# Where the squares of a projection's tiles are added up: matmul engine or pool engine

## The chip, the cores and the metric

The kernel runs on one core of one Trainium2 chip. The metric is the device time of one execution, in microseconds (us). The kernel before takes 815.71 us, the median of 3 runs (815.12 to 815.75).

## The reference, cut to what matters

A sequence of 256 tokens with 16 extra tokens in front of it, 1024 channels wide, in float32, passes through two blocks. The first block is a feed-forward network, an mLSTM mixer and a second feed-forward network; the second block is two layers of dilated attention beside a gated convolution. Every part ends in the same way: an output projection, an RMS norm of its result with a gain per channel, and an addition to the stream h.

```python
h = h + 0.5 * rmsnorm(swiglu(rmsnorm(h, gn[0]), ffn_w_in[i, 0], ffn_w_out[i, 0]), gn[1])
u = rmsnorm(h, gn[2])
y = mlstm_mixer(u, ...)                    # ends in: y @ w_out
h = h + rmsnorm(y, gn[3])                  # the first output projection of the change
h = h + 0.5 * rmsnorm(swiglu(rmsnorm(h, gn[4]), ffn_w_in[i, 1], ffn_w_out[i, 1]), gn[5])
# then, for l in 0, 1
mix = jnp.concatenate([att, cnv], axis=-1) @ w_out[l]
x = x + gate[:, None, :] * rms_norm(mix, post_norm_g[l])   # l = 0: the second one of the change
```

`rmsnorm(y, g)` needs, for each token, the sum over the 1024 channels of y². The kernel also wants the norm of the *next* part without waiting for the new h: the mean of (h + r·g·y)² is the mean of h² + 2r·mean(h·g·y) + r²·mean(g²·y²), where r is the first norm's factor. So at each boundary three sums per token are formed: of y², of (g·y)² and of h·g·y.

## The kernel before, in words

Channels lie on the 128 partitions and tokens on the free axis: h is `hT`, 8 tiles of 128 channels by 272 tokens. A weight chunk is 128 x 1024 floats. It arrives by DMA in `raw` (5 slots), and `advance` (L189) splits it into a high part `w1`, copied by ScalarE (ACT), and a low part `w2`, which VectorE (DVE) gets by a subtraction of two SBUF operands (`w<-raw,w`). Each product takes three matmuls, w1·x1, w1·x2 and w2·x1. A block of 128 output channels over 8 input tiles is thus 24 matmuls of 256 tokens. `advance` is called ahead of use: when block j is issued, the split of the chunk four further on goes into the queues of ACT and DVE.

The kernel's order is written out by hand. Each engine has one list (`Eng`, whose `replay` is the line L110 or L112 of nearly every instruction in the profile), is served in that order, and waits for semaphores of the others. TensorE (PE) runs the matmuls, GpSimd is called POOL here, and SyncE (SP) issues the DMAs.

An output projection is `row_of_tiles` (L279). For the feed-forward networks it has 22 input tiles for each of 8 output tiles; for the mixers it has 8. In the mixers' case `head` (L233) does the first three output tiles together, ending one right after the other, and `block` (L264) does one at a time after that. A block can call a function in its middle, `mid`, before its seventh input tile (after 18 of its 24 matmuls).

After each output tile k, `evac_tile` (L399) reads it from PSUM `ps`. In all cases ACT writes g·y into `yg`, and DVE multiplies it by h (`hyg`) and adds that to the running `sqa[2]`. For the squares there are two ways.

- *Row sums on PE* (not `pooled`: both mixers' projections). ACT writes y² into `sq`. `column_sums` (L384) then makes `sq` the stationary operand of a small matmul per 128 tokens, against two columns of `wts`: 1/D and g²/D. So one square serves both sums. A float32 matmul is two PE instructions, so that a tile's row sums are four. They wait in the list `late` and are issued in the middle of the next block; those of the last tile follow its square.
- *Gathered on POOL* (`pooled`: both feed-forward networks). ACT writes two squares, of y into `sq` and of g·y into `sqg`. POOL adds each into a running sum, `sqa[0]` and `sqa[1]`. `early_sums` (L459) sums both over the partitions, in eight small PE instructions, in the middle of the last tile. There PE waits for POOL's additions of the seventh tile. For the last tile only y² is formed and summed with both weights.

After the last tile, `rms_first` (L485) reads the sums, POOL takes the power -1/2, and PE spreads the factor over the partitions (`spread`, L478). Then `add_and_weigh` (L608, after the mixer) or `add_and_normalise` (L579, layer 0) updates h and makes the operands of the next `head`. `dense` issues filler matmuls for waits of PE.

The queues of DVE and ACT in a mixer's projection, from tile 3 on, are: for each block the split of a chunk, then the evacuation of that block's tile. The split that is queued with block 7 stands in front of the evacuation of tile 7. Ahead of tile 3's evacuation stand the splits of three chunks (numbered 5, 6, 7, counting the projection's own from 0), the first of which block 5 needs. The chunks up to 11 are split by the end of the projection.

Of the kernel before, what the change touches and what calls it, by code (L numbers as in the profile page):

```python
# [17 lines left out]
S = 256  # L18
# [96 lines left out]
def build(nc, xT, wst, wada, vec, cst, tab, rb, outT):  # L115
    ctx = ExitStack()
    with ctx:
# [37 lines left out]
        ps = ctx.enter_context(nc.psum_tensor("ps", [P, 8, 512], F32))  # L155
# [57 lines left out]
        free = {b: None for b in range(8)}  # L213
# [50 lines left out]
        def block(x1, x2, n, mid=None, at=KT - 2, ahead=NW - 1):  # L264

            if ready:
                return ready.pop(0)
            b = take()
            c = chunk(ahead)
            pe.wait(free[b])  # L270
            for kt in range(KT):
                if mid and kt == at:
                    mid()
                m = tile_products(ps[:, b, 0:n], c, kt, x1[:, kt, :], x2[:, kt, :], kt == 0, kt == KT - 1,
                                  kt == KT - 1)
            done_chunk(c, m)
            return b, m
# [451 lines left out]
        W_MIX = 6  # L729
# [163 lines left out]
        ygm = ffn(T, lambda j: gh[:, j:j + 1], None, hm, 0, w_ffn[0])  # L893
# [40 lines left out]
        b, m = block(x1, x2, T)  # L934
# [56 lines left out]
        for j in range(8):  # L991
            i = j % 2
            b, m = block(x1, x2, T)
# [6 lines left out]
            b, m = block(x1, x2, T)  # L1000
# [126 lines left out]
        ygm = {}  # L1127
# [6 lines left out]

        def evac_mix(gain, ygm, paired=True):
            def evac(j, b, mk_):
                free[b] = ygm[j] = evac_tile(ps[:, b, 0:S], S, 16, j, gain(j), None, mk_, paired)
            return evac

        row_of_tiles(KT, KT, y1, y2, S, evac_mix(vg(3), ygm), (yw1, yw, range(KT), last_outputs))  # L1140
# [2 lines left out]
        ygm = ffn(S, lambda j: gh[:, 8 + j:9 + j], guard, hm, 16, w_ffn[1], hook)  # L1143
# [288 lines left out]
        ygm, hm = layer(0, ygm, hm)  # L1432
# [93 lines left out]
```

How the kernel before makes its waits and increments, by code:

```python
    def replay(self, eng):  # L105
        for fn, m in self.ops:
            if fn is None:
                eng.wait_ge(m[0], m[1])
            elif m is None:
                fn()
            else:
                fn().then_inc(m[0], m[1])
```

## Time and profile before

| what | value |
|---|---|
| median of 3 runs | 815.71 us (815.12 to 815.75) |
| the profiled execution | 816.1 us |
| its span in the profile | 814.3 us |
| PE busy | 801.9 us, 98% |
| DVE busy | 592.0 us, 73% |
| ACT busy | 417.1 us, 51% |
| POOL busy | 144.2 us, 18% |
| mean granted TensorE clock | 0.995 |

The span is from the first instruction to the last. A busy share is an average over all stages. The mixer's projection runs from about 316 to 343 us of the span and layer 0's from about 648 to 674 us; the projections of the feed-forward networks end at about 213 and 537 us.

### The profile page before, as it was taken

The page shows a single profiled execution, that of the slowest core. Times are in us where ns is not written, and L with a number is a line of the kernel's source. Part 1 is how long each engine was busy: PE and PEld are TensorE (multiplying, and loading weights), DVE is VectorE, ACT ScalarE, POOL GpSimd, SP SyncE. Part 2 cuts the span into 40 slices and gives each one's busy share as a digit, 9 for nine tenths or more (in the row PEclk, how much of TensorE's full clock was granted, in tenths as well). Part 3 has the DMA queues.
Part 4 walks back from the last instruction along what each step waited for, and adds up shares of the span by engine and source line. Part 5 has one row for each costly group of instructions (what it writes and reads, how often), then busy time and mean ns, then how long its engine had stood idle before and what let it go on. Part 6 is the DMA issues. An engine that isn't in the chain of part 4 may idle for free.

```text
span 814.3 us, 15551 instructions
## 1 busy us (share of the span) xinstructions
PE 801.9 (98%) x6350; PEld 775.7 (95%) x6350; DVE 592.0 (73%) x958; ACT 417.1 (51%) x710; POOL 144.2 (18%) x156
## 2 busy tenths in 40 slices
PE   9999999999999999999999999999999999999997
PEld 9999999999899999999999999999899999999986
DVE  6777766798687875788777779976667567567753
ACT  7544444445267565555444455436555454555541
POOL 3800000032220000020000004230245302035510
PEclk9999999999999999999999999999999999999999
DMA  9876776686336643458867779535544651744531
GB/s 335 302 257 220 237 251 237 217 298 191 104 118 207 197 122 101 155 178 291 282 230 261 253 231 341 184 105 207 153 158 129 183 161 47 258 156 131 155 104 52
DMA packets 45191, 158.84 MB, mean 195 GB/s; under 512 B 5040, under 2 KB 6576, under 8 KB 45120
## 3 DMA queue, kind: packets, MB, share of 16 engines
q1 hardware_dynamic: 45120, 157.85, 58.5%
q8 instruction: 50, 0.82, 0.4%
q14 instruction: 21, 0.17, 0.1%
HBM read 156.76 MB, written 1.06 MB: 194 GB/s over the span
## 4 chain that ended last, share of the span: by engine, by line
PE 80%; DVE 11%; ACT 5%; issue 3%; POOL 1%; DVEq 0%; POOLq 0%; ACTq 0%
PE ps L110 72%; PE ps L112 8%; DVE w L112 3%; ACT w L112 2%; DVE u L112 2%; DVE tmp L112 1%; DVE yg L112 1%; DVE cv L112 1%; ACT SW L112 1%; ACT L112 1%; ACT ytm L112 1%; POOL rst L112 1%; DVE Vs L112 0%; DVE g L112 0%; POOL hT L112 0%
## 5 line engine op out<-in xcount | busy, mean ns | idle before, releaser
L110 PE MATMUL ps<-u,w 128*128 128x256 f32 (+1 forms) x3887 | 502.1, 285 | 2.8 <-ACT u L112 0.8
L110 PEld LDWEIGHTS ps<-u,w 128*128 128x128 f32 x3887 | 483.0, 189 | 12.2 <-issue 2.8
L112 DVE TENSOR_TENSOR w<-raw,w 128x1024 fp32r<-128x1024 f32 x245 | 297.5, 1226 | 141.9 <-ACT w L112 141.5
L112 ACT CAST w<-raw 128x1024 fp32r<-128x1024 f32 x245 | 254.0, 1048 | 127.3 <-PE ps L112 121.8
L110 PE MATMUL ps<-h,w 128*128 128x272 f32 (+1 forms) x1000 | 130.0, 285 | 0.0
L110 PEld LDWEIGHTS ps<-h,w 128*128 128x128 f32 x1000 | 125.7, 188 | 0.1
L112 POOL TENSOR_TENSOR sqa<-sqa,sq 128x272 f32<-128x272 f32 (+1 forms) x16 | 20.7, 1294 | 322.4 <-ACT sq L112 322.0
L112 POOL TENSOR_SCALAR Sb<-Sb,st 128x256 f32<-128x256 f32 x32 | 45.0, 1424 | 89.1 <-DVE st L112 89.1
L112 DVE SCALAR_TENSOR_TENSOR acc<-adr,cact,acc 128x1024 f32<-128x1024 f32 x42 | 57.7, 1398 | 0.0
L112 ACT ACTIVATE si<-tmp 128x272 f32<-128x272 f32 (+1 forms) x44 | 18.7, 424 | 70.0 <-DVE tmp L112 70.0
L112 PE MATMUL ps<-u,w 128*128 128x256 f32 (+1 forms) x169 | 48.1, 285 | 0.0
L112 POOL TENSOR_TENSOR rst<-sst,eps 128x2 f32<-128x2 f32 (+3 forms) x8 | 6.1, 761 | 177.8 <-DVE sums L112 153.3
L112 DVE TENSOR_TENSOR hf<-si,ps 128x272 f32<-128x272 f32 (+1 forms) x44 | 18.9, 430 | 21.1 <-ACT si L112 21.1
L112 PEld LDWEIGHTS ps<-u,w 128*128 128x128 f32 x169 | 32.1, 190 | 0.0
L112 ACT ACTIVATE sq<-ps 128x256 f32<-128x256 f32 (+1 forms) x30 | 11.6, 388 | 32.0 <-PE ps L112 31.8
L112 ACT ACTIVATE Sb<-Sb,st 128x256 f32<-128x256 f32 x32 | 16.0, 502 | 16.8 <-DVE st L112 16.8
L110 PE MATMUL ps<-y,w 128*128 128x256 f32 x184 | 24.5, 285 | 0.0
L110 PE MATMUL ps<-m,w 128*128 128x256 f32 x184 | 24.3, 285 | 0.0
L110 PEld LDWEIGHTS ps<-m,w 128*128 128x128 f32 x184 | 22.9, 192 | 0.0
L110 PEld LDWEIGHTS ps<-y,w 128*128 128x128 f32 x184 | 22.8, 189 | 0.0
L110 PE MATMUL ps<-w,u 128*128 128x512 f32 x88 | 21.7, 394 | 0.0
L112 POOL TENSOR_TENSOR hT<-hT,yg 128x256 f32<-128x256 f32 (+1 forms) x23 | 17.7, 770 | 21.4 <-DVE yg L112 21.4
(185 smaller groups left out, 746.8 us busy)
## 6 DMA issues: line engine op xcount, KB each, us to landing
raw<-wst SPq DMA_DIRECT2D x245, 512.0 KB, 4.6
adr<-wada SPq DMA_DIRECT2D x48, 512.0 KB, 4.1
Bt<-bias_rows SPq DMA_DIRECT2D x8, 192.0 KB
hT<-xT SPq DMA_DIRECT2D x4, 272.0 KB, 5.4
outT<-yg SPq DMA_DIRECT2D x4, 256.0 KB, 2.1
cs<-cst SPq DMA_DIRECT2D x1, 140.0 KB, 5.3
cs<-cst SPq DMA_DIRECT2D x1, 128.0 KB, 7.2
vc<-vec SPq DMA_DIRECT2D x1, 101.0 KB, 3.6
```

The costliest lines, as they stand in the source:

```text
L110: fn()
L112: fn().then_inc(m[0], m[1])
```

## The change

One argument changes. With the pair of columns of `wts` in the place of `None`, `evac_tile` takes the pooled way in both mixers' projections, as it does in the feed-forward networks:

```diff
         def evac_mix(gain, ygm, paired=True):
             def evac(j, b, mk_):
-                free[b] = ygm[j] = evac_tile(ps[:, b, 0:S], S, 16, j, gain(j), None, mk_, paired)
+                free[b] = ygm[j] = evac_tile(ps[:, b, 0:S], S, 16, j, gain(j), (W_MIX + 14, W_MIX + 16), mk_,
+                                                 paired)
             return evac
```

These are the lines of `evac_tile` that now run for tiles 0 to 6, and what is issued in the middle of the last block:

```python
if k == 0 and pooled:
    state["ya"] = act(Square, sqa[:, 0, 0:n] <- src)
    if paired:
        state["ga"] = act(Square with scale gain, sqa[:, 1, 0:n] <- src)
...
elif 0 < k and not last:
    sqr[i] = state["ya"] = pool(sqa[:, 0] += sq[:, i], q, state["ya"])
    if paired:
        q = act(Square with scale gain, sqg[:, i2] <- src, sgr[i2])
        sgr[i2] = state["ga"] = pool(sqa[:, 1] += sqg[:, i2], q, state["ga"])
...
def early_sums(n, paired):
    if "ya" in state:
        column_sums(7, sqa[:, 0, :], n, W_ONE, SUM_Y, True, False, state.pop("ya"))
        if paired:
            state["early"] = column_sums(7, sqa[:, 1, :], n, W_ONE, SUM_G, False, False, state["ga"])
```

`late` stays empty, so only the last block calls `early_sums`. The last tile's own sums, against both columns, stay as they were. The change occurs twice in the program, at the mixer's projection and at layer 0's.

## Rows read from the trace of the kernel before

**Rows 1.** The page: busy us, share of the span and instructions of each engine.
```profile
PE 801.9 (98%) x6350; PEld 775.7 (95%) x6350; DVE 592.0 (73%) x958; ACT 417.1 (51%) x710; POOL 144.2 (18%) x156
```

**Rows 2.** Chain of waits in order of time: start us, us, what.
```profile
332.73 2.25 PE ps L110 x20
...
336.02 2.25 PE ps L110 x20
...
342.62 0.39 ACT sq L112
```

**Rows 3.** Timeline, mixer's projection, PE: start, us, engine, line, op, tiles, shape, count.
```profile
325.11 2.29 PE L110 MATMUL ps<-y,w 128*128 128x256 f32 x18
327.24 0.28 PE L110 MATMUL ps<-wts,sq 128*128 128x2 f32 x2
...
328.49 0.83 PE L110 MATMUL ps<-y,w 128*128 128x256 f32 x5
...
343.58 0.38 PE L110 MATMUL ps<-wts,hyg 128*128 128x1 f32 x2
...
344.70 0.69 PE L112 MATMUL ps<-cs,rst 128*128 128x128 f32 x2
```

**Rows 4.** Groups of instructions by form, VectorE, 325.2 to 343.5 us: count | busy us, mean ns | idle before.
```profile
L112 DVE TENSOR_TENSOR w<-raw,w 128x1024 fp32r<-128x1024 f32 x7 | 8.4, 1221 | 0.2
L112 DVE TENSOR_TENSOR sqa<-sqa,hyg 128x256 f32<-128x256 f32 x6 | 2.6, 426 | 0.2
L112 DVE TENSOR_TENSOR hyg<-yg,hT 128x256 f32<-128x256 f32 x6 | 2.5, 424 | 3.0 <-ACT yg L112 3.0
```

**Rows 5.** Timeline, mixer's projection, VectorE.
```profile
325.38 0.43 DVE L112 TENSOR_TENSOR sqa<-yg,hT 128x256 f32<-128x256 f32 x1 [3.01 <-ACT yg L112]
...
341.06 1.23 DVE L112 TENSOR_TENSOR w<-raw,w 128x1024 fp32r<-128x1024 f32 x1
...
343.04 0.48 DVE L112 SCALAR_TENSOR_TENSOR hyg<-ps,vc,hT 128x256 f32<-128x256 f32 x1 [0.76 <-ACT sq L112]
```

**Rows 6.** Timeline, mixer's projection, ScalarE.
```profile
324.60 0.38 ACT L112 ACTIVATE sq<-ps 128x256 f32<-128x256 f32 x1 [2.68 <-PE ps L112]
...
326.48 2.98 ACT L112 CAST w<-raw 128x1024 fp32r<-128x1024 f32 x3
```

**Rows 7.** Timeline, second feed-forward network's projection, ScalarE.
```profile
504.80 0.39 ACT L112 ACTIVATE sq<-ps 128x256 f32<-128x256 f32 x1 [1.59 <-PE ps L112]
...
505.44 0.48 ACT L112 ACTIVATE yg<-ps,gh 128x256 f32<-128x256 f32 x1
```

**Rows 8.** Timeline, the same projection, GpSimd and VectorE.
```profile
511.25 4.04 DVE L112 TENSOR_TENSOR w<-raw,w 128x1024 fp32r<-128x1024 f32 x3
513.10 1.10 POOL L112 TENSOR_TENSOR sqa<-sqa,sq 128x256 f32<-128x256 f32 x1 [4.36 <-ACT sq L112]
514.16 1.72 POOL L112 TENSOR_TENSOR sqa<-sqa,sqg 128x256 f32<-128x256 f32 x1
...
528.73 1.23 DVE L112 TENSOR_TENSOR w<-raw,w 128x1024 fp32r<-128x1024 f32 x1 [1.36 <-ACT w L112]
529.05 1.50 POOL L112 TENSOR_TENSOR sqa<-sqa,sq 128x256 f32<-128x256 f32 x1 [5.87 <-ACT sq L112]
530.51 0.74 POOL L112 TENSOR_TENSOR sqa<-sqa,sqg 128x256 f32<-128x256 f32 x1
530.70 0.82 DVE L112 TENSOR_TENSOR hyg<-yg,hT 128x256 f32<-128x256 f32 x1
```

**Rows 9.** Timeline, layer 0's projection, ScalarE (its first tile) and TensorE (its last).
```profile
655.79 0.38 ACT L112 ACTIVATE sq<-ps 128x256 f32<-128x256 f32 x1 [4.88 <-PE ps L112]
...
674.95 0.38 PE L110 MATMUL ps<-wts,hyg 128*128 128x1 f32 x2
```

**Rows 10.** Windows: stretch, busy us of PE, PEld, DVE, ACT, POOL, granted clock, DMA, GB/s.
```profile
345.00:346.00 1.00, 1.00 (x6) 1.00 (x5) 0.54 (x2) 0.00 (x0) 0.00 (x0) 0.50 0.00 0
...
348.00:349.00 1.00, 1.00 (x10) 1.00 (x10) 0.96 (x4) 0.14 (x1) 0.82 (x1) 1.00 0.99 401
```

## The prediction

> **What bounds the kernel now.** I read the page first: PE is busy for 98% of the span and POOL for 18% [rows 1]. That invites moving work from PE to POOL, but it is an average over stages. The chain of waits shows what decides in the mixer's projection. From 328 us to 342.6 it consists of PE alone, in blocks 3.28 us apart (332.73 to 336.02), and then passes to ACT's square of the last tile [rows 2]. PE's timeline prices a block's parts: 18 product matmuls take 2.13 us (325.11 to 327.24), so 24 take 2.84; the row sums of three tiles take 1.25 us (327.24 to 328.49) [rows 3]. The rest of a block, 3.28 - 2.84 = 0.44 us, is one tile's row sums. The groups and timelines of DVE then show what it holds in the same stretch: seven chunk splits of 1.22 us and thirteen products and additions of 0.43 us, all with both operands in SBUF [rows 4, 5]. For DVE alone that fits. The second feed-forward network's projection shows what happens once POOL adds beside such work, and the estimate rests on that [rows 8].
>
> **What the change takes off PE.** Seven tiles' row sums go: 1.25 for tiles 0 to 2 and 4 x 0.44 for tiles 3 to 6, together 3.0 us. Two column sums come in the last block, 2 x 0.44 = 0.88. PE saves 2.1 us a projection, 4.3 us for both, if nothing else moves.
>
> **What it adds to ACT.** Per tile 0 to 6 one more square, with a gain. The two squares take 0.64 us before the next instruction starts (504.80 to 505.44) [rows 7], against 0.28 for the plain one, so the extra one is 0.36. For the first three tiles, which come at once, ACT needs 1.88 us now (324.60 to 326.48) and will need about 3.0, so its three copies begin at 327.6 in place of 326.48 and, at 2.98 us, end at 330.6 [rows 6]. Per later block ACT has 0.64 + 0.36 + about 1 us for a copy, 2 of 2.84 us. That is hidden.
>
> **What it adds to POOL, and through it to DVE.** Twelve additions of 128x256 per projection, on an idle POOL. Alone one would take 0.74 us (530.51), 8.9 in all. But they don't run alone. At 529.05 an addition starts while DVE subtracts (528.73 to 529.96). It ends at 530.55, 0.59 after DVE's end. The next holds POOL until 531.25; DVE's product started at 530.70 and ends at 531.52, 0.82 us in place of 0.43, 0.27 after POOL's end. At 513.10 an addition ends at 514.20; DVE's third subtraction, due by 513.6, ends at 515.29 with its two predecessors (4.04 us for three), 1.09 after POOL, and POOL's next one ends at 515.88, again 0.59 after DVE [rows 8]. So two-operand work from SBUF on DVE and an addition on POOL exclude each other for whole instructions, and they take turns: 0.59 us for an addition, 1.09 for a split, about 0.3 for a small DVE instruction.
>
> The Trainium skill says the same, against this change (SBUF — State Buffer, "Who interferes with whom"): a DVE instruction with two SBUF inputs contends with a GpSimd instruction that reads SBUF, and the later one is blocked until the other is through. The trace agrees, by the 0.82 us above. Were there no such rule, the sum would be the first rival's.
>
> The common queue then holds per tile 0.59 x 2 + 1.09 + 0.3 x 2 = 2.87 us, against 2.84 of PE: no room. And it starts full, since three tiles come at once. From DVE's first product (325.38 + 0.36 for ACT's extra square = about 325.75) I let them take turns; s is a split (by chunk), p and a are DVE's product and addition, y and g POOL's two additions (by tile), each with the time at which it ends:
> p0 326.2, y1 326.8, p1 327.1, g1 327.7, a1 328.0, y2 328.6, p2 328.9, g2 329.5, a2 329.8, s5 331.0; tile 3's square is there at 330.9: y3 331.6, s6 332.7, g3 333.3, s7 334.4, y4 335.0, p3 335.3, g4 335.9, a3 336.2, y5 336.8, s8 337.9, g5 338.5, p4 338.8, y6 339.4, a4 339.7, g6 340.3.
> POOL is through. DVE still has s9, p5, a5, s10, p6, a6 and s11 ahead of the last tile's product: 3 x 1.12 + 4 x 0.37 = 4.8 us (durations of [rows 4], less the 0.05 to 0.1 by which starts overlap ends). That product, on which the last sums wait, starts at 345.1. Today it is at 343.04 [rows 5].
>
> **PE in the same time.** Without row sums it ends tile 3 at 327.95 and tile 4 at 330.8, waits 0.2 for s5, ends tile 6 at 336.7 and is in the middle of block 7 at 338.8. It waits for y6 (0.6), sums 0.44, waits for g6 (0.5), sums 0.44 and ends at 341.5, 1 us earlier than now. It gains nothing by that, because behind it stands the last sum of h·g·y, which needs a6 (about 344.1) and then the last product. What is late next is DVE.
>
> **What follows on the path.** The last product's sums start at 345.65 in place of 343.58. Then come four fillers, and the first spread at 346.6 in place of 344.70 [rows 3]: +1.9 us. DVE's and POOL's work behind it is unchanged. In layer 0 ACT's first square is at 655.79, 331.2 later, and the same queue follows; the last product's sums would come at 676.85, now 674.95 [rows 9]: +1.9. Behind both boundaries PE is dense again for a long way, and nothing gives the time back. The next chunks' DMAs are released by splits up to 2 us later, but the chunks split by then serve the next head's first blocks, so I put this at nothing (without that cover, 1 us each).
>
> Sum: +3.8 us. The profiled execution took 816.1 us for a span of 814.3, 0.4 above the median; 816.1 + 3.8 = 819.9 there, and 815.7 + 3.8 = 819.5 as the median.
>
> Bounds per projection: from below, the queue without a gap and with the shortest turns (13 x 0.27 + 7 x 1.09 + 12 x 0.59 = 18.2 from 325.75) puts the product at 344.0, +0.9. From above, full durations at the end (3 x 1.22 + 4 x 0.43) and 0.05 lost at each of 24 turns give +0.6 + 1.2, so +3.7. I take 1.9, the walk.
>
> **PE's clock.** It is at 1.2 GHz from about 344.6 to 348 already (granted 0.50 in 345 to 346, 1.00 in 348 to 349) [rows 10], after three tiles' and then each tile's row sums and the small sums of the end. It will now idle from 341.5 to 344.1. The stretch behind is bound by DVE and POOL after the mixer, and by fillers and spreads after layer 0. I count nothing, and -0.5 to +0.7 each.
>
> **The rivals.**
> *Gain on PE decides.* DVE keeps up, the last product comes straight after PE's last tile: -2.1 each, 811.4 us. For it: DVE is idle in every block now (its later products wait 3.0 us in all for `yg`) [rows 4]. Against it: rows 8, which leave no overlap. Chance 0.10.
> *A draw.* The turns cost less than they should, because copies or squares arrive so that DVE and POOL miss each other; the delay eats the gain and little more, +0.7 each at most: 814.2 to 817.1. For it: the order in which they meet is my guess; only the sum of the work is sure. Chance 0.10.
> *The clock falls for longer.* This is slower than the forecast: PE idles or sums for nearly 5 us at each end, and stays at the lower level into the next head. Row sums went on at full clock for three blocks, so an idle stretch is what differs. If 3.4 us more of PE-bound matmuls run at half speed, each boundary costs 1.7 us more: 823. It decides only if the stretch reaches beyond the DVE-bound part. Chance 0.08. The Trainium skill (TensorE: Matmul & The Clock Gate, "What's actually happening") holds that throttled is the default and activity releases it, which is this rival's rule; the trace's 0.50 at 345 us agrees with it as far as it goes.
> *DVE and POOL in turn, as walked*: 819.5 us, own range 817.3 to 822. Chance 0.72.
>
> About 0.2% (1.6 us) is what a measurement can tell from no change. Faster by more: 0.10. Within: the draw's lower part and the forecast's edge, 0.09. Slower: 0.81. For 8 in 10 I leave out the first rival and the extremes: 816.6 to 822.4.
>
> **What would show it.** Right: no row sums between blocks, blocks 2.84 apart; POOL additions of 1 to 1.7 us in 326 to 341; DVE products of 0.7 to 0.8 us; splits running on after PE has ended, and the last product near 345; PE waiting for DVE `sqa` about 2.6 us, for POOL `sqa` about 1 us. The later stages must be shifted and not stretched. Wrong: additions of 0.74 us throughout, or the last product within 0.7 us of PE's last tile.

## The result, and the profile after

The changed kernel takes 821.15 us (median of 6 runs, 820.79 to 823.97), the kernel before, measured beside it, 815.6 us (6 runs, 814.82 to 815.95). The medians are 5.5 us apart, a ratio of 1.0068. The ratio over all runs is 1.0075, 95% interval [1.0065, 1.0086]; the one run of 823.97 weighs in it. Forecast were 819.5 us, +3.8, and 816.6 to 822.4 as the range. The span of its profile is 819.4 us, against 814.3.

The page after has PE as busy as before and POOL at 21% in place of 18% [rows 1]. Its one hint at a loss is that DVE is busy for 9.7 us more with the same 958 instructions.

```profile
PE 802.8 (98%) x6310; PEld 775.6 (95%) x6310; DVE 601.7 (73%) x958; ACT 421.6 (51%) x724; POOL 171.6 (21%) x180
```

PE's timeline in the mixer's projection, as in [rows 3]; what stands in brackets is PE's idle time before the line, and who ended it:

```profile
324.96 2.89 PE L110 MATMUL ps<-y,w 128*128 128x256 f32 x23
327.80 2.89 PE L110 MATMUL ps<-y,w 128*128 128x256 f32 x23
...
339.47 0.38 PE L110 MATMUL ps<-wts,sqa 128*128 128x1 f32 x2 [0.55 <-POOL sqa L112]
...
341.14 0.38 PE L110 MATMUL ps<-wts,sqa 128*128 128x1 f32 x2 [1.06 <-POOL sqa L112]
...
343.81 0.47 PE L110 MATMUL ps<-wts,sqa 128*128 128x1 f32 x2 [1.25 <-DVE sqa L112]
...
345.42 0.57 PE L110 MATMUL ps<-wts,hyg 128*128 128x1 f32 x2
...
347.27 0.63 PE L112 MATMUL ps<-cs,rst 128*128 128x128 f32 x2
```

The row sums between the blocks are gone and blocks stand 2.84 us apart. Then PE waits twice for POOL's totals and once for DVE's. GpSimd's timeline shows the additions behind those waits, and VectorE's what they meet (as in [rows 5] and [rows 8]):

```profile
326.61 1.01 POOL L112 TENSOR_TENSOR sqa<-sqa,sqg 128x256 f32<-128x256 f32 x1
...
334.17 0.93 POOL L112 TENSOR_TENSOR sqa<-sqa,sq 128x256 f32<-128x256 f32 x1
335.06 0.92 POOL L112 TENSOR_TENSOR sqa<-sqa,sqg 128x256 f32<-128x256 f32 x1
335.94 1.73 POOL L112 TENSOR_TENSOR sqa<-sqa,sq 128x256 f32<-128x256 f32 x1
...
339.38 1.70 POOL L112 TENSOR_TENSOR sqa<-sqa,sqg 128x256 f32<-128x256 f32 x1
```

```profile
327.06 0.84 DVE L112 TENSOR_TENSOR sqa<-sqa,hyg 128x256 f32<-128x256 f32 x1
...
333.54 0.96 DVE L112 TENSOR_TENSOR hyg<-yg,hT 128x256 f32<-128x256 f32 x1
334.53 0.85 DVE L112 TENSOR_TENSOR sqa<-sqa,hyg 128x256 f32<-128x256 f32 x1
335.30 1.76 DVE L112 TENSOR_TENSOR w<-raw,w 128x1024 fp32r<-128x1024 f32 x1
...
343.67 1.22 DVE L112 TENSOR_TENSOR w<-raw,w 128x1024 fp32r<-128x1024 f32 x1
344.81 0.48 DVE L112 SCALAR_TENSOR_TENSOR hyg<-ps,vc,hT 128x256 f32<-128x256 f32 x1
```

Read the two fences as one. POOL's addition that starts at 334.17 ends at 335.10, DVE's at 335.38 (0.28 later), POOL's next one at 335.98 (0.60 later), DVE's split at 337.06 (1.08 later), POOL's next at 337.67 (0.61 later). Each engine's record holds the other's work. DVE's 0.43 us instructions last 0.84 to 0.97 and its 1.22 us splits 1.74 to 1.76, until POOL is through at 341.08. The product of the last tile, on which the boundary waits, starts at 344.81. I call it the last product. In layer 0 it starts at 674.41 before and at 678.68 after; before, then after:

```profile
674.41 0.48 DVE L112 SCALAR_TENSOR_TENSOR hyg<-ps,GP,hT 128x256 f32<-128x256 f32 x1 [0.79 <-ACT sq L112]
...
678.87 0.48 DVE L112 SCALAR_TENSOR_TENSOR tmp<-hT,G,ps 128x256 f32<-128x256 f32 x1 [0.67 <-PE ps L112]
```

```profile
678.68 0.48 DVE L112 SCALAR_TENSOR_TENSOR hyg<-ps,GP,hT 128x256 f32<-128x256 f32 x1
...
683.95 0.48 DVE L112 SCALAR_TENSOR_TENSOR tmp<-hT,G,ps 128x256 f32<-128x256 f32 x1 [0.71 <-PE ps L112]
```

The chain of waits at the end of this projection (start, us, what) goes through DVE's backlog and then through PE's small matmuls:

```profile
341.76 1.20 DVE w L112
342.96 0.35 DVE hyg L112
...
343.33 0.43 DVE sqa L112
...
343.81 0.47 PE ps L110 x2
344.28 0.43 PE ps L112 x2
...
346.41 1.06 PE ps L110 x4
347.47 0.44 PE ps L112 x2
```

Before, two such PE instructions took 0.22 us (334.98 in the chain of before: `0.22 PE ps L112 x2`) and now 0.43. The windows (columns as in [rows 10]) tell why: TensorE is granted 0.50 from 344 us on, its 1.2 GHz level, until 350.8, and from 675.1 to 685.3 at layer 0, there already ahead of the last block's last six products; before it was at that level from 344.6 to 348 and from 675.7 to 679.1.

```profile
344.00:345.00 1.00, 1.00 (x7) 1.00 (x6) 1.00 (x2) 0.00 (x0) 0.00 (x0) 0.50 0.71 180
...
349.00:350.00 1.00, 0.77 (x3) 0.59 (x3) 0.97 (x4) 0.72 (x2) 0.00 (x0) 0.50 0.57 156
...
351.00:352.00 1.00, 1.00 (x11) 1.00 (x10) 0.93 (x5) 0.51 (x1) 0.33 (x1) 1.00 1.01 414
```

**Where the 5.1 us of the spans are.** I count from the start of block 3 of each projection (before 325.11 and 656.32, after 324.96 and 658.83). The last product starts 17.93 us after it before and 19.85 after in the mixer; 18.09 and 19.85 in layer 0. From there to DVE's first instruction with the spread factor it is 2.38 and 3.13 us in the mixer. From there to DVE's first `tmp<-hT` it is 4.46 and 5.27 in layer 0. So DVE's delay makes 1.92 + 1.76 = 3.7 us and what follows it 0.75 + 0.81 = 1.6. Together these are 5.2; the mixer's block 3 came 0.15 earlier. The profiled execution of the kernel before is 0.5 us slower than the median of its runs, which is the rest of the way to 5.5.

### The profile page after: what moved, and what is told of

Its sections match the earlier page's. It is cut to its first block, busy times and chain, and to the rows that moved or that the text cites. A ratio compares the mean times of both kernels' runs of the same rounds, so it can differ in the third digit from the quotient of the medians.

```text
span 819.4 us, 15530 instructions
## 1 busy us (share of the span) xinstructions
PE 802.8 (98%) x6310; PEld 775.6 (95%) x6310; DVE 601.7 (73%) x958; ACT 421.6 (51%) x724; POOL 171.6 (21%) x180
## 3 DMA queue, kind: packets, MB, share of 16 engines
HBM read 156.76 MB, written 1.06 MB: 193 GB/s over the span
## 4 chain that ended last, share of the span: by engine, by line
PE 77%; DVE 12%; ACT 6%; issue 3%; POOL 1%; DVEq 0%; POOLq 0%; ACTq 0%
PE ps L110 69%; PE ps L112 8%; DVE w L112 4%; ACT w L112 2%; DVE u L112 2%; DVE tmp L112 1%; DVE yg L112 1%; DVE cv L112 1%; ACT SW L112 1%; ACT L112 1%; ACT ytm L112 1%; POOL rst L112 1%; DVE hyg L112 1%; ACT yg L112 0%; DVE Vs L112 0%
## 5 line engine op out<-in xcount | busy, mean ns | idle before, releaser
L112 DVE TENSOR_TENSOR w<-raw,w 128x1024 fp32r<-128x1024 f32 x245 | 300.6, 1239 | 141.3 <-ACT w L112 141.2
L112 ACT CAST w<-raw 128x1024 fp32r<-128x1024 f32 x245 | 254.8, 1052 | 127.4 <-PE ps L112 123.2
L112 POOL TENSOR_TENSOR sqa<-sqa,sq 128x256 f32<-128x256 f32 (+1 forms) x28 | 34.6, 1236 | 426.0 <-ACT sq L112 425.6
L112 POOL TENSOR_SCALAR Sb<-Sb,st 128x256 f32<-128x256 f32 x32 | 45.0, 1422 | 89.2 <-DVE st L112 89.2
L112 DVE SCALAR_TENSOR_TENSOR acc<-adr,cact,acc 128x1024 f32<-128x1024 f32 x42 | 57.7, 1397 | 0.0
L112 ACT ACTIVATE si<-tmp 128x272 f32<-128x272 f32 (+1 forms) x44 | 18.7, 424 | 70.0 <-DVE tmp L112 70.0
L112 PE MATMUL ps<-u,w 128*128 128x256 f32 (+1 forms) x169 | 48.1, 285 | 0.0
L112 DVE TENSOR_TENSOR hf<-si,ps 128x272 f32<-128x272 f32 (+1 forms) x44 | 18.9, 430 | 21.1 <-ACT si L112 21.1
L112 PEld LDWEIGHTS ps<-u,w 128*128 128x128 f32 x169 | 32.1, 190 | 0.0
L112 POOL TENSOR_TENSOR sqa<-sqa,sqg 128x256 f32<-128x256 f32 (+1 forms) x24 | 30.3, 1262 | 0.0
L112 ACT ACTIVATE Sb<-Sb,st 128x256 f32<-128x256 f32 x32 | 16.0, 502 | 16.8 <-DVE st L112 16.8
L112 ACT ACTIVATE sq<-ps 128x256 f32<-128x256 f32 (+1 forms) x28 | 11.5, 410 | 21.2 <-PE ps L112 21.2
L112 POOL TENSOR_TENSOR hT<-hT,yg 128x256 f32<-128x256 f32 (+1 forms) x23 | 17.6, 769 | 22.6 <-DVE yg L112 22.6
```

Source lines behind the costliest of these rows:

```text
L112: fn().then_inc(m[0], m[1])
```

## Experiments

Each kernel was measured beside the kernel before, which took 815.06 us in the first set (9 runs; the four experiments up to "sums behind") and 815.26 us in the second (28 runs; the others). "Product" is the start of the last product after block 3 in the mixer, "first use" the start of DVE's `yg<-yg,ps` behind it, in us; both are read from one profiled execution each. The row "changed" is from the result above.

| kernel | median | ratio to before, 95% interval | product | first use |
|---|---|---|---|---|
| before | | 1 | 17.93 | 20.31 |
| changed | 821.15 | 1.0075 [1.0065, 1.0086] | 19.85 | 22.98 |
| POOL only writes | 810.81 | 0.9948 [0.9934, 0.9961] | 15.71 | 17.84 |
| fillers | 818.06 | 1.0038 [1.0025, 1.0050] | 19.88 | 21.85 |
| product from PSUM | 818.46 | 1.0045 [1.0033, 1.0058] | 18.55 | 21.97 |
| sums behind | 820.90 | 1.0073 [1.0060, 1.0085] | 19.86 | 23.11 |
| five tiles, product from PSUM | 812.98 | 0.9971 [0.9959, 0.9982] | 16.92 | 19.11 |
| five tiles | 814.35 | 0.9992 [0.9983, 1.0000] | 17.83 | 20.12 |
| all tiles, from PSUM, sums behind | 814.57 | 0.9995 [0.9987, 1.0004] | 17.72 | 20.78 |
| before with fillers | 815.24 | 0.9999 [0.9990, 1.0008] | 17.93 | 20.12 |

### POOL only writes

```diff
-pool(tensor_tensor, sqa[:, 0, 0:n], sqa[:, 0, 0:n], sq[:, i, 0:n], ALU.add)      # and sqa[:, 1] with sqg
+pool(memset, sqa[:, 0, 0:n], 1.0)                                               # same waits, mixers only
```

> The changed kernel, but in the two mixers' projections POOL's 24 additions are replaced by memsets of the same 128x256 part of sqa: they wait for the same squares, are waited for by the same sums, and read nothing from SBUF. The squares are thus not added up there. Theory A (DVE and POOL exclude each other because both read SBUF through something they share): DVE is no longer held up, its products take 0.42 us and not 0.85 to 0.97, the last product starts about 0.6 us after PE's last tile, and the full gain on PE shows: 2 x 2.1 us below the kernel before, 811.4 us (810.6 to 812.6). Rival B (the later squares on ACT, or the mere order and waits of the new queue, delay the last tile): ACT's load and all waits are unchanged, so it stays at 819 to 821.

Measured: 810.81 us, 4.25 below the kernel before. This kernel leaves the adding up of the squares out and is no version to use. POOL's and DVE's timelines, from tile 1 on, and the last product:

```profile
326.28 0.68 POOL L112 MEMSET sqa<- 128x256 f32 x2 [0.33 <-ACT sq L112]
...
330.12 0.68 POOL L112 MEMSET sqa<- 128x256 f32 x2 [3.17 <-ACT sq L112]
```

```profile
326.44 0.42 DVE L112 TENSOR_TENSOR sqa<-sqa,hyg 128x256 f32<-128x256 f32 x1
...
327.92 3.50 DVE L112 TENSOR_TENSOR w<-raw,w 128x1024 fp32r<-128x1024 f32 x3
331.33 0.42 DVE L112 TENSOR_TENSOR hyg<-yg,hT 128x256 f32<-128x256 f32 x1
...
340.05 0.48 DVE L112 SCALAR_TENSOR_TENSOR hyg<-ps,vc,hT 128x256 f32<-128x256 f32 x1 [0.83 <-ACT sq L112]
```

The memsets run under DVE's addition and under its splits, and neither engine is held up. The same number of POOL instructions, the same squares on ACT and the same waits are left; only the reading and its longer duration are gone. With them went 10 us. ACT's extra squares and the new order cost nothing (rival B falls), and what PE saves is worth the 2.1 us a projection that was counted: the last product starts 2.22 us earlier after block 3 in the mixer and 2.19 in layer 0. A memset is also shorter than an addition (two in 0.68 us, against 0.74 for one). But mere length isn't the cause: DVE's addition at 326.44 lies wholly inside two memsets and takes 0.42 us, where the changed kernel's, beside an addition on POOL, took 0.84 (at 327.06).

### Fillers

```diff
 def early_sums(n, paired):
+    dense(4)                                  # mixers only, all three
     column_sums(7, sqa[:, 0, :], ...)
+    dense(9)
     column_sums(7, sqa[:, 1, :], ...)
 ...
+    dense(12)
     state["early"] = column_sums(5, sqa[:, 2, :], ...)
```

> The changed kernel with filler matmuls on PE where it waits in the mixers' projections: 4 ahead of the wait for the sum of y2, 9 ahead of that of the gained squares, 12 ahead of the last sum of h*g*y. DVE and POOL work as in the changed kernel. Theory C (the part of the loss that the walk did not hold, 0.7 us per boundary, is the last sums, fillers and spreads at 1.2 GHz): the granted clock stays at 1.00 from 343 to 348 us, the sums take 0.22 us per two instructions and not 0.43, and the time is 1.0 to 1.5 us below the changed kernel's 821.2: 819.7 to 820.2. Rival D (the walk underrated the turns of DVE and POOL): the time stays at 821 or rises by the fillers that are in the way, up to 822.

Measured: 818.06 us, 3.0 above the kernel before, where the change has 5.5 to 6. The last product is where it was (19.88), and from it to the first use 1.97 us pass in place of 3.13. PE's timeline and a window:

```profile
344.88 0.38 PE L110 MATMUL ps<-wts,hyg 128*128 128x1 f32 x2 [0.48 <-DVE hyg L112]
345.12 0.36 PE L112 MATMUL ps<-wts,hyg 128*128 128x1 f32 x2
```

```profile
342.00:346.00 4.00, 3.52 (x30) 3.41 (x30) 3.08 (x8) 0.86 (x2) 0.70 (x1) 1.00 0.69 230
```

The theory held and was too small. The clock at 1.2 GHz costs the changed kernel about 1.2 us at the mixer's boundary and, by the distance from block 3 to `tmp<-hT` (23.59 against 25.12), 1.5 at layer 0's, not 0.7 each. I had taken the difference to the kernel before, which pays for its own fall and has one thing more ahead of its spread: there the sums of the last square come just ahead of those of the last product, while here they are done before that product starts. Rival D falls: with the clock kept, what is left is DVE's delay.

### The product from PSUM

```diff
-c = dve(tensor_tensor, hyg, y, h, ALU.mult)                                 # two operands from SBUF
+c = dve(scalar_tensor_tensor, hyg, src, gain, h, ALU.mult, ALU.mult)        # src in PSUM, h in SBUF
+free[b] = c                                                                 # the bank, tiles 0 to 6
```

> The changed kernel, but DVE's product h*g*y of tiles 0 to 6 in the mixers' projections reads PSUM, the gain and hT in one instruction (one SBUF operand, as the last tile's product already does) in place of yg and hT (two SBUF operands). Each PSUM bank is released by that product. Theory A: the product no longer takes a turn with POOL: it takes 0.4 to 0.5 us whatever POOL does, and six turns of about 0.3 us leave the common queue, so the last product starts 1.5 to 2 us earlier (about 343) and the time is 3 to 4 us below the changed kernel, 817.3 to 818.3. Rival E (the delay is DVE's own load): the product is 0.05 us longer than before, so 821 to 822.

Measured: 818.46 us, 2.4 below the changed kernel by the ratios (1.0045 against 1.0075 of 815). DVE's timeline, then POOL's, then PE's:

```profile
335.46 0.48 DVE L112 SCALAR_TENSOR_TENSOR hyg<-ps,vc,hT 128x256 f32<-128x256 f32 x1
335.97 0.45 DVE L112 TENSOR_TENSOR sqa<-sqa,hyg 128x256 f32<-128x256 f32 x1
336.34 1.76 DVE L112 TENSOR_TENSOR w<-raw,w 128x1024 fp32r<-128x1024 f32 x1
...
343.44 0.48 DVE L112 SCALAR_TENSOR_TENSOR hyg<-ps,vc,hT 128x256 f32<-128x256 f32 x1 [0.80 <-ACT sq L112]
```

```profile
334.42 1.72 POOL L112 TENSOR_TENSOR sqa<-sqa,sqg 128x256 f32<-128x256 f32 x1
```

```profile
341.28 0.38 PE L110 MATMUL ps<-wts,sqa 128*128 128x1 f32 x2 [1.06 <-POOL sqa L112]
```

The product takes its 0.48 us at 335.46, while POOL's addition (until 336.14) is under way. An instruction 0.05 us longer in itself made DVE faster, so rival E falls. The run changes two things at once, the operand and the form of the instruction (`SCALAR_TENSOR_TENSOR` for `TENSOR_TENSOR`). The kernel before tells them apart, at layer 0's boundary, where DVE runs that form with either kind of operand beside POOL's addition to `hT`:

```profile
679.60 0.47 DVE L112 SCALAR_TENSOR_TENSOR tmp<-hT,G,ps 128x256 f32<-128x256 f32 x1
679.99 0.78 DVE L112 SCALAR_TENSOR_TENSOR u<-tmp,mod,u 128x256 fp32r<-128x256 f32 x1
...
683.30 0.48 DVE L112 SCALAR_TENSOR_TENSOR u<-tmp,mod,u 128x256 fp32r<-128x256 f32 x1
```

```profile
679.76 0.73 POOL L112 TENSOR_TENSOR hT<-hT,yg 128x256 f32<-128x256 f32 x1 [0.76 <-DVE yg L112]
```

With one operand from PSUM (`ps`) it takes 0.47 us, and POOL, which starts in the middle of it, is not held up (0.73). With both tensors in SBUF (`tmp` and `u`) it ends 0.28 us after POOL and takes 0.78, against 0.48 beside an idle POOL. So the operand decides, not the form.

The gain is smaller than forecast, because the last product now waits for ACT's square of the last tile, and that for PE, which loses 1.07 and 1.06 us to POOL in the middle of the last block: a new wait in the place of the old one. The clock also falls earlier here, at 342.2 us: from the product to the first use it takes 3.42 us in place of 3.13, so that the first use gains 1.0 of the product's 1.3.

### Sums behind the last tile

```diff
 def early_sums(n, paired, behind=False):
-    if "ya" in state:
+    if "ya" in state and (behind or not mixer):
 ...
+    early_sums(n, paired, True)               # after the last tile's matmuls
     state["early"] = column_sums(5, sqa[:, 2, :], ...)
```

> The changed kernel with the two column sums of POOL's totals issued behind the last tile's matmuls in place of the middle of the last block, in the mixers' projections. PE no longer waits 0.55 + 1.06 us for POOL inside the block. Theory A (what comes last is DVE's last product, near 344.8 us): nothing is gained, 820.7 to 821.6; the last tile ends at about 339.5 instead of 342.4 and PE waits that much longer for DVE. Rival F (PE's waits for POOL are themselves the price): 1.6 us less per boundary, 818 us.

Measured: 820.90 us, no different from the change. The last tile's matmuls end at 339.2, and PE then waits:

```profile
343.52 0.59 PE L110 MATMUL ps<-wts,sqa 128*128 128x1 f32 x2 [2.07 <-DVE sqa L112]
```

PE's 1.6 us of waiting for POOL inside the block, the most visible new entry in its list of waits, cost nothing while DVE was later still. Rival F falls.

### Fewer additions: three versions

With two prices known I ran what they point to. Tiles 5 and 6 go back to row sums on PE:

```diff
-pooled = not paired or gw
+pooled = not paired or (gw and not (mixer and 4 < k < KT - 1))   # early_sums ahead of the rows in late
```

Five tiles, with the product from PSUM and three fillers:

> Only tiles 0 to 4 of the mixers' projections are gathered on POOL (8 additions in place of 12), tiles 5 and 6 have row sums on PE in the next block as before the change; DVE's products read PSUM; 3 filler matmuls stand ahead of the last sum of h*g*y. Theory A: PE saves 1.25 us a boundary, the four additions that go are those that stood latest in the common queue, so DVE is ready when PE's last tile ends (last product about 16.6 us after the start of block 3, against 17.9 before the change and 19.9 with it), and with the clock kept it is 1.3 + 0.4 us a boundary below the kernel before: 811.5 to 812.8. Rival (the turns still delay DVE): 814 to 816.

Five tiles, with the product from SBUF and four fillers:

> As the kernel with tiles 0 to 4 gathered on POOL, but DVE's products read yg and hT from SBUF as in the changed kernel, and 4 fillers. Theory A (each addition holds DVE up for its 0.59 us): the last product comes 4 x 0.59 = 2.4 us earlier than with the change, about 17.5 us after the start of block 3, which is 0.4 to 0.5 below the kernel before, and 0.4 more by the clock: 1.8 us below it in all, 813.0 to 814.2. Rival (what counts is PE's saving alone): the same as the kernel with products from PSUM, 812.

All seven tiles, from PSUM, sums behind, nine fillers:

> All seven tiles gathered on POOL; DVE's products read PSUM; the two column sums of POOL's totals stand behind the last tile, with 9 fillers between them. Theory A: DVE's queue ends about 17.7 us after the start of block 3 (it did so with the products from PSUM), 0.2 below the kernel before, PE no longer waits inside the block, and the clock is kept (0.4 us a boundary): 0.6 us a boundary below the kernel before, 813.5 to 815. Rival (PE's waits for POOL decide again): 816 to 817.

Measured: 812.98, 814.35 and 814.57 us. The first beats both kernels, by 2.3 us or 0.29% against the kernel before, and its interval lies wholly below 1. It is less than the 2.5 to 3.8 us forecast: the product comes 1.0 earlier than before and not 1.3, as PE still waits 0.16 for POOL and fills in front of the sums. DVE's timeline:

```profile
341.48 0.48 DVE L112 SCALAR_TENSOR_TENSOR hyg<-ps,vc,hT 128x256 f32<-128x256 f32 x1 [0.27 <-ACT sq L112]
```

DVE had to wait for that tile, so it is no longer the bound.

With the product from SBUF, four additions fewer bring the last product 2.02 us forward, from 19.85 to 17.83, of the 2.4 expected. With all tiles and the product from PSUM it is at 17.72, as forecast, with nobody waiting in the block. But in the profiled execution the fillers did not keep the clock (0.50 from 343 us on): its first use comes 0.47 us later than in the kernel before. That execution is the slowest of the version's eleven (816.59 us and a mean granted clock of 0.991; the others 813.75 to 816.36 and 0.993 to 1.000), so its profile shows the version at its worst. That version and five tiles from SBUF can't be told from the kernel before.

### The kernel before, with fillers

```diff
     state["early"] = column_sums(5, sqa[:, 2, :], ...)
+    dense(3)                                  # mixers only
```

> The kernel before with 3 filler matmuls in each mixer's projection while PE waits for the square of the last tile. Theory C (the kernel before loses 0.3 to 0.4 us a boundary because its spread runs at 1.2 GHz): if three fillers are enough to keep the clock, 0.5 to 0.8 us below the kernel before; if the row sums are what lets it fall, the clock still falls near 344.6 us and the time is 0 to 0.4 us above.

Measured: 815.24 us, a ratio of 0.9999. The clock stays at 1.00 behind both projections, and the first use comes only 0.2 us earlier (20.12), since the fillers delay the last square's sums (DVE's read of them is 0.73 us behind the product, not 0.66). At layer 0 the distance from block 3 to `tmp<-hT` is 22.14 against 22.55. Within the profiles the fillers thus give back 0.6 us, as theory C had it; the medians don't show it, but their interval is 0.7 us wide to either side, and the kernel before doesn't always pay. Of its 28 runs the ten with a granted clock of 0.999 or more have a median of 814.8 us, the others 815.4. So fillers alone don't give the 2.3 us of the version of five tiles; whether it keeps its clock without its three was not run.

## Why the prediction was right, and where its size was off

**What bounds, and what moves.** Right. PE was the bound; with the row sums gone DVE was later than PE, and the loss is where it was put.

**PE's saving, 2.1 us a projection.** Right: the run in which POOL only writes shows 4.25 us for both, against 4.3. PE's own end was off. Forecast were 341.5 us for its last tile, about 1 us of waiting for POOL and 2.6 for DVE; it ended near 342.5, on the same scale, and waited 1.6 and 1.25, because POOL ended later than walked. That cost nothing, as DVE was later still.

**ACT's extra squares.** Right: hidden. They shift the first splits, as said.

**DVE and POOL in turns.** Right, nearly line by line. With the measured times moved by the 0.15 us between the two starts of block 3:

| end of, in the mixer | walked | measured + 0.15 |
|---|---|---|
| tile 2, last DVE addition | 329.8 | 329.8 |
| split 5, for which PE waits | 331.0 | 331.0 |
| tile 3, POOL's second addition | 333.3 | 334.4 |
| split 7 | 334.4 | 333.8 |
| tile 5, POOL's second addition | 338.5 | 338.7 |
| tile 6, POOL's second addition | 340.3 | 341.2 |
| start of the last product | 345.1 | 345.0 |

The order of the turns was wrong in one place, and POOL ended 0.9 us later. POOL's addition of tile 3 came a moment after the second split had begun, not before it. But DVE's backlog was then smaller, and the sum of all turns fixed the end, as the draw's rival had it: "only the sum of the work is sure". The price of a turn was read from four rows of another stage [rows 8], and the changed kernel repeats them: 0.60, 0.28 and 1.08. The run with the product from PSUM, and the two operand kinds beside POOL in the kernel before, show that this is exclusion and that an operand decides it. The term measured 1.92 and 1.76 us, 3.7 for both, against the forecast's 3.8. That fit is in part luck: the walk's last product is 2.06 us later than today's, and the forecast then wrote 1.9 for the mixer's spread without a reason, so that its own walk makes 4.0.

**What follows on the path: the term that was mis-sized.** "I count nothing, and -0.5 to +0.7 each" for PE's clock. What follows the last product measured +0.75 and +0.81. The step that failed is the sentence before it, that the stretch behind is bound by DVE and POOL after the mixer. That is so from the first use on. Ahead of it stand the product's four small sum instructions, four fillers and the spread, all on PE, one behind another, and the forecast moved their rows as they stood before, at 0.22 us per pair of sums. Now a pair took 0.43, the two pairs 0.85 us in place of 0.46, and from the fillers' start to the spread's it was 1.00 in place of 0.66. In the mixer PE had waited 2.9 us for POOL and DVE before them; in layer 0 it had waited 1.5 for POOL when the clock fell. By the runs with fillers the fall costs the changed kernel 1.16 and 1.56 us (3.13 against 1.97, 5.27 against 3.71) and the kernel before 0.19 and 0.42 (2.38 against 2.19, 4.46 against 4.04). The clock's own term is thus +1.0 and +1.1 where -0.5 to +0.7 was allowed, and 0.2 and 0.3 of it come back because the last square's sums no longer stand in the way. The forecast's 3.8 and this 1.6 make 5.4, against 5.5 between the medians. The third rival named the cause, but put the price into the next head, where nothing was lost: behind the mixer's first use the chain is the same length as before.

**The gain on PE decides; a draw.** Neither. The first is what the kernel would do if POOL did not read SBUF.

**DMAs and later stages at nothing.** Right: from the first use on both kernels run the same chain; from DVE's `yg<-yg,ps` to the next dense stretch of PE it takes 14.18 us before (345.42 to 359.60) and 14.16 after (347.94 to 362.10). From there to block 3 of layer 0 it is 296.7 us in both.

## What to carry to other kernels

Before work goes to an idle POOL, list what DVE runs meanwhile with two operands in SBUF, add both engines' durations into one queue, and compare it with the time there is: here 2.84 to 2.87 us per tile, by the measured and the forecast turns, against 2.84, behind a queue that starts full. Where it doesn't fit, let DVE take one operand from PSUM, or move only as many tiles as the queue holds; both together, with three fillers, gained 0.29% where the whole move lost 0.75%. And where a delay makes PE idle just ahead of small matmuls that somebody waits for, count those at both clock levels.

## What the runs showed of the hardware that was not expected

The clock's fall depends on more than the idle time. With all tiles from PSUM and sums behind, PE was never idle for more than 0.4 us between 339 and 344, ran nine fillers and many sums of one column, and still was at 0.50 from 343; the kernel of five tiles, with three fillers, stayed at 1.00 over both boundaries. In five tiles from SBUF it fell behind the mixer (0.50 from 344 to 347) and not behind layer 0. What separates these cases the runs leave open. Part of it doesn't lie in the kernel. Behind the first feed-forward network all ten programs are the same, and PE's rows from 212 to 216 us have the same lengths to 0.01 us. Two of the ten profiles (product from PSUM, before with fillers) are at 0.50 from 216 to 222.8 all the same, and the other eight stay at 1.00. A window of the kernel before with fillers, then one of the kernel before:

```profile
216.00:222.00 6.00, 5.43 (x24) 4.78 (x24) 5.13 (x16) 1.25 (x3) 3.14 (x4) 0.50 0.01 1
```

```profile
216.00:222.00 6.00, 4.72 (x30) 3.66 (x30) 5.45 (x17) 1.26 (x3) 3.16 (x4) 1.00 0.00 1
```

So one profile doesn't show that a version keeps or loses its clock. For the change it is plain even so: its six runs have mean granted clocks of 0.985 to 0.991, the 28 of the kernel before 0.993 to 1.000.

An execution's early part varies: block 3 of the mixer started between 324.34 and 325.40 us in ten profiles whose code up to that projection is the same. Distances within a profile were therefore compared, not its times.
